# The delta rule of the fourth layer: chunk-sized tiles on quarters of the array, its steps between the projections

## The reference

```python
def gated_deltanet_mixer(h, w_in, conv_w, a_log, dt_bias, o_norm, w_out):
    proj = h @ w_in
    qkv = jax.nn.silu(causal_dwconv(proj[..., :GDN_QKV_W], conv_w))
    ...
    o = gated_delta_chunked(q, k, v.reshape(B, S, GDN_HEADS, GDN_DV), g, beta)
    o = gated_rmsnorm(o, gate.reshape(B, S, GDN_HEADS, GDN_DV), o_norm).astype(h.dtype)
    return o.reshape(B, S, GDN_V_W) @ w_out

# inside gated_delta_chunked, for each chunk of C = 64 tokens
    a = jnp.where(strict, jnp.einsum('nbhid,nbhjd->nbhij', k_beta, kc) * decay, 0.0)
    t_mat = lax.linalg.triangular_solve(a + eye, ...)
    w_val = t_mat @ v_beta
    k_cum = t_mat @ (k_beta * jnp.exp(gc)[..., None])
    attn = jnp.einsum('nbhid,nbhjd->nbhij', qc, kc) * decay
    def step(state, xs):
        v_new = w_i - jnp.einsum('bhcd,bhdv->bhcv', kc_i, state)
        o_i = jnp.einsum('bhcd,bhdv->bhcv', q_i, state) + jnp.einsum('bhij,bhjv->bhiv', at_i, v_new)
        state = state * dl_i[..., None, None] + jnp.einsum('bhcd,bhcv->bhdv', ke_i, v_new)
```

## Time and profile before

| | us |
|---|---|
| median of 3 runs (3168.34 to 3177.97) | 3168.7 |
| the profiled execution | 3162.18 |
| its span, from the first to the last instruction | 3160.9 |
| mean granted TensorE clock | 0.967 of full speed |
| odd mixer in that span | 2168.3 to 2536.5 |

### The profile page before, as it was taken

How to read it: one execution, slowest core, us unless ns; L and a number is a source line. 1 busy time by engine, 2 the same in 40 slices (tenths; PEclk the granted TensorE clock), 3 DMA queues, 4 the chain that set the end, 5 groups by cost and what they waited for, 6 DMA issues and landing times.

```text
span 3160.9 us, 40792 instructions
## 1 busy us (share of the span) xinstructions
PE 2919.8 (92%) x15750; PEld 2079.9 (66%) x15750; DVE 1179.3 (37%) x2588; ACT 480.9 (15%) x1051; POOL 102.7 (3%) x98
## 2 busy tenths in 40 slices
PE   7998899999998899999999999998968789999998
PEld 5666678787666688887755555556868665555554
DVE  2435324433435324442344222225475244222223
ACT  2222301001222311001211111111310111111111
POOL 0000000000000000000010000000000001000000
PEclk9998899999998899999999999999979889999999
DMA  5222146563222146654459999993300229999995
GB/s 186 77 80 74 60 143 242 201 250 106 80 80 80 54 161 240 251 208 157 165 215 395 404 401 400 410 401 139 133 14 1 111 116 409 398 405 404 392 394 228
DMA packets 104979, 684.59 MB, mean 217 GB/s; under 512 B 17760, under 2 KB 19312, under 8 KB 24496
## 3 DMA queue, kind: packets, MB, share of 16 engines
q1 hardware_dynamic: 93040, 665.22, 53.6%
q0 software_dynamic: 11264, 16.54, 1.5%
q10 hardware_dynamic: 576, 1.43, 0.1%
HBM read 703.57 MB, written 4.19 MB: 224 GB/s over the span
## 4 chain that ended last, share of the span: by engine, by line
PE 79%; DMA 10%; DVE 6%; ACT 2%; issue 1%; SPq 0%; DVEq 0%; ACTq 0%; POOLq 0%
PE PS L454 75%; DMA wmoe<-in_experts 10%; PE PS L459 4%; ACT AR L2114 1%; DMA COLS<-in_cols 0%; ACT AR L2164 0%; SPq L2663 0%; DVE wmoe L1826 0%; DVE H L1826 0%; DMA AR<-tokens,IX 0%; ACT ST L2114 0%; DVE ST L1304 0%; DVE wmoe L1324 0%; ACT wmoe L2114 0%; DVE wmoe L1834 0%
## 5 line engine op out<-in xcount | busy, mean ns | idle before, releaser
L454 PE MATMUL PS<-wmoe,AR 128*64 128x256 f32 (+1 forms) x5360 | 716.0, 423 | 33.4 <-DMA wmoe<-in_experts 22.1
L454 PE MATMUL PS<-H,wdense 128*128 128x256 f32 (+1 forms) x3056 | 713.8, 394 | 9.1 <-DVE H L1334 3.6
L454 PEld LDWEIGHTS PS<-H,wdense 128*128 128x128 f32 x3056 | 587.0, 194 | 119.3 <-issue 15.1
L454 PEld LDWEIGHTS PS<-wmoe,AR 128*64 128x64 f32 x5360 | 384.2, 137 | 317.2 <-issue 142.3
L2114 ACT ACTIVATE AR<-PS 128x256 f32<-128x256 f32 (+4 forms) x512 | 231.9, 457 | 1706.6 <-PE PS L454 1100.9
L454 PE MATMUL PS<-AR,wdense 128*128 128x256 f32 (+1 forms) x1920 | 440.4, 389 | 28.9 <-DVE AR L1864 9.8
L454 PE MATMUL PS<-AR 128*128 128x512 f32 (+13 forms) x1492 | 401.4, 408 | 48.3 <-DVE AR L1311 13.8
L454 PEld LDWEIGHTS PS<-AR,wdense 128*128 128x128 f32 x1920 | 367.3, 192 | 95.8 <-issue 20.4
L454 PEld LDWEIGHTS PS<-AR 128*128 128x128 f32 (+6 forms) x1492 | 209.1, 189 | 147.7 <-issue 90.5
L459 PEld LDWEIGHTS PS<-CST,AR 128*128 128x128 f32 (+5 forms) x1158 | 131.8, 135 | 167.1 <-issue 137.8
L454 PE MATMUL PS<-wdense,H 128*128 128x256 f32 (+4 forms) x1024 | 219.7, 371 | 0.0
(11 more groups left out here) (286 smaller groups left out, 1541.6 us busy)
## 6 DMA issues: line engine op xcount, KB each, us to landing
wmoe<-in_experts SPq DMA_DIRECT2D x402, 1024.0 KB, 8.8
wdense<-in_dense SPq DMA_DIRECT2D x176, 1024.0 KB, 4.8
wmoe<-in_ada SPq DMA_DIRECT2D x48, 1024.0 KB, 7.0
tokens<-AR POOLq DMA_DIRECT2D x4, 512.0 KB, 3.4
wdense<-in_dense SPq DMA_DIRECT2D x2, 768.0 KB, 10.5
CST<-in_const SPq DMA_DIRECT2D x1, 1389.0 KB, 19.7
wdense<-in_dense SPq DMA_DIRECT2D x2, 640.0 KB, 6.3
AR<-tokens,IX POOLq DMA_INDIRECT x71, 7.8
```

The costliest lines, as they stand in the source:

```text
L454: return te.matmul(out, lhsT, rhs, start=start, stop=stop, skip_group_check=True)
```

## The change

The tiles of the mixer become half as wide. A matrix of a head is 64 x 64 for each chunk, and the two chunks of a tile lie one above the other on the partitions (`[P, 8, CH]`), so an operation of VectorE or ScalarE covers all eight heads in 512 elements. `by_chunk` forms a product of all heads as 16 products of 64 x 64, chunk 0 on rows and columns 0 to 63 of the array and chunk 1 on rows and columns 64 to 127, into one bank. The masks and identities in the constants are cut to that width.

```diff
+            def by_chunk(what, lhs, rhs, *readers):
+
+                o = bank(what, *readers)
+                for j in range(8):
+                    for r0 in (0, CH):
+                        m = mm(o[r0:r0 + CH, j * CH:(j + 1) * CH], lhs(j, slice(r0, r0 + CH)), rhs(j, slice(r0, r0 + CH)))
+                PE.up(m, *what)
```

```diff
+                for s in range(1, 6):
+                    te.wait_ge(VE.sem, VE.of("ti", t, s - 1))
+                    by_chunk(("ax", t, s), lambda j, r: AM[r, j, :], lambda j, r: TI[r, j, :], AC)
+                    yield
+                    te.wait_ge(VE.sem, VE.of("tt", t, s - 1))
+                    te.wait_ge(AC.sem, AC.of("ax", t, s))
+                    if s < 5:
+                        by_chunk(("ti", t, s), lambda j, r: TT[r, j, :], lambda j, r: XX[r, j, :], VE)
+                    by_chunk(("tt", t, s), lambda j, r: XX[r, j, :], lambda j, r: TT[r, j, :], VE)
+                    yield
+                te.wait_ge(VE.sem, VE.of("tt", t, 5))
+                both = [bank(("kct", t, r), reader(r)) for r in range(2)]
```

```diff
+                    for j in range(8):
...
+                    yield
+                    o = bank(("odd o", t, r), VE)
+                    if n > 0:
+                        te.wait_ge(VE.sem, VE.of("kct", t, 0))
+                        te.wait_ge(AC.sem, AC.of("kct", t, 1))
+                        te.wait_ge(VE.sem, VE.of("state", n - 1))
```

```diff
+    def odd_order(ba, qkv, silu, qk, p0, p1, v0, v1, gate, gated, chunks, out):
+
+        return in_turn((ba, 1), (qkv, 2), (ba, 1), (qkv, 1), (p0, 1), (p1, 1), (qkv, 1), (silu, 1), (p0, 1), (qkv, 1), (p0, 1),
...
-    parts += wide("od_w_in_2", 0, 0, 16) + wide("od_w_in_2", 0, 4096, 1, step=16) + wide("od_w_out_2", 0, 0, 4)
+    parts += wide("od_w_in_2", 0, 4096, 1, step=16) + wide("od_w_in_2", 0, 0, 16) + wide("od_w_out_2", 0, 0, 4)
...
-        sp.wait_ge(PES[1].sem, PES[1].of("kv", 1, 1))
-        sp.wait_ge(VES[1].sem, VES[1].of("kv", 1, 1, 1))
+        sp.wait_ge(PES[1].sem, PES[1].of("odd o", 1, 1))
```

More of the change, by code:

```diff
@@ L928, in odd_mixer @@
         def odd_mixer():
-            steps = feature_steps(("odd qkv",), H, DC, S, 12, lambda j: AC, ("odd h",))
-            run(steps)
-            norms = norm_heads(("odd qk",), 4, [O_MIX[:, 0:4, :], O_MIX[:, 4:8, :]])
-            for j, _ in enumerate(feature_steps(("odd gate",), H, DC, S, 4, lambda j: reader(j))):
-                if j % 2 == 1:
-                    advance(norms, 1)
-            run(norms)
-            slot = take(DC, 16)
-            o = bank(("ba",), VE)
-            for t in range(2):
-                m = sum_k(o[:, 16 * t:16 * t + 16], [H[:, k, t * P:(t + 1) * P] for k in range(DC)], [slot[:, k, :] for k in range(DC)])
@@ new lines, in out @@
+            def out():
+                for n in range(4):
+                    yield
+                    te.wait_ge(AC.sem, AC.of("odd", "squared", n))
+                    o = bank(("odd", "sums", n), AC)
+                    PE.up(mm(o, ones, O_SQ[n % 2]), "odd", "sums", n)
+                    yield
+                    yield
+            nothing = iter(())
+            run(odd_order(decay_inputs(), feature_steps(("odd qkv",), H, DC, S, 12, lambda j: AC), nothing, qk_norms(),
+                          prepare(0), prepare(1), v_turned(0), v_turned(1),
+                          feature_steps(("odd gate",), H, DC, S, 4, lambda j: AC), nothing, chunks(), out()))
@@ L1865, in odd_mixer @@
+            nothing = iter(())
+            run(odd_order(decay_inputs(), convolved(), silu(), qk_norms(), prepare(0), prepare(1), v_turned(0), v_turned(1), nothing,
+                          gated(), chunks(), out()))
             mix_out(L, "odd out")
@@ L2419, in odd_mixer @@
-            norms = norm_heads(("odd qk",), fours[0:4], halves, 1, lambda j: ("silu", 5) if j < 2 else ("odd qk normed", j - 2))
-            for _ in odd_steps(("odd gate",), 8, lambda c, o: (O_GATE[:, c, :], o[:, 0:S])):
-                advance(norms, 1)
-            run(norms)
-            ac.wait_ge(VE.sem, VE.of("ba"))
-            AC.up(act(O_BETA, O_BA[:, :, 0:8], Sigmoid), "beta")
-            ac.preload_act_table_set("natural_log_exp_and_others")
-            AC.up(act(O_EA, row("od_a_log_2", 0, 8), Exp), "decay rate")
@@ L2466, in odd_mixer, with gated @@
-            ac.preload_act_table_set("natural_log_exp_and_others")
+            def gated():
+                for t in range(2):
+                    ac.wait_ge(PE.sem, PE.of("v turned", t, 1))
+                own()
+                for q in range(2):
+                    AC.up(act(O_KV[:, 8 + 4 * q:12 + 4 * q, :], O_GATE[:, 4 * q:4 * q + 4, :], Sigmoid), "odd gate", "sigmoid", q)
+                ac.preload_act_table_set("natural_log_exp_and_others")
+                yield
+                yield
@@ L2467, in odd_mixer @@
+            nothing = iter(())
+            run(odd_order(decay_inputs(), raw(), silu(), qk_norms(), prepare(0), prepare(1), nothing, nothing,
+                          all_steps(("odd gate",), 8, lambda c, o: (O_GATE[:, c, :], o[:, 0:S])), gated(), chunks(), out()))
             layer_norm("odd ln")
```

533 lines of the change are left out of this document (319 added, 214 removed).

## The result

The changed kernel takes 3071.5 us (median of 4 runs, 3070.82 to 3072.53) against 3168.5 for the kernel before on the same chip (4 runs, 3166.02 to 3177.97): a ratio of 0.9689, 95% interval 0.9669 to 0.9709. The forecast was 3047 with a range of 3032 to 3084. The kernel became 97 us faster where 122 were forecast.

The account below looks back on a forecast made before the run. It took the fourth mixer as bound by steps waiting between TensorE and VectorE. Output projection 119.7 us earlier plus 2.4 from its clock gave -122.1 against the 3168.7 median: 3046.6, said as 3047, range 3032 to 3084.

Parts of the forecast that it names:

- Quarter passes at 0.025 us, 38 x 0.80 = 30.4: Solve and what feeds it: 38 groups of 32 quarter passes at 0.80 us each, 30.4 us of TensorE.
- Chunks 33.4 us at full clock: Chunk stage: 16 blocks of 16 passes at 1.8, three sums of 0.86 and 2.0 between array shapes, no wait.
- Beta and decay 6.4, three columns 10.35: Mixer's start: 32 beta and decay passes take 6.4 us, then projection columns at 3.45 us each.
- Output projection 6.9 instead of 9.34: Behind the mixer: first 32 passes, 9.34 us at a lowered clock, take 6.9 with TensorE busy; 2.4 us gained.
- Waits 3.3 and 1.5: TensorE waits 3.3 us before the first solve product, 1.5 before the first state product behind VectorE's two gate multiplies.
- Tail 4.1: After the last chunk output: square, sums, logarithm, exponential and one multiply, 4.1 us before the output projection.
- the seams: Entering another array shape: 0.20 us for about 15 entries before the chunks (3.0), 0.1 for about 20 inside (2.0).
- Vector work of 105 us under 168: Mixer before the chunks: about 105 us of vector work under 168 of TensorE, so VectorE no longer bounds.
- Loads at nothing: Expert weight loads: the later queue wait (89 us instead of 109) and the small beta slot cost nothing.
- B: Rival: two quarters writing one bank do not overlap in the 38 solve groups; +31 us, 3078; chance 0.18.
- C: Rival: late copies or convolutions at about half the solve's twelve hand-overs, 2.5 us each; +15, 3062; chance 0.15.
- D: Rival: small quarter products lower the clock, whole mixer at 1.2 GHz; 237 us more, 3284, slower; chance 0.03.

Follow-up runs that it names:

- the order experiment: Changed kernel with each group's products issued for all heads of tokens 0 to 63 first, then 64 to 127, instead of in pairs: 3092.6 us, ratio 0.9765.

## Why the prediction came out as it did

**The mechanism was right, the clock was not.** The idle time of the solve went, the experts' layer kept its length, the granted clock was 1.00 from 2205 to 2365, and the range held the result. The measured mixer is 98.9 us shorter instead of 119.7, and the output projection behind it gained nothing instead of 2.4. That is 23.2 of the 25 us missing between the medians. The profiled execution's mixer began 11.2 us later than before's, which belongs to the layers ahead (the mixer of the third layer begins 4.9 us later already).

**What the steps measured, against the terms of the sum:**
- *Quarter passes at 0.025 us, 38 x 0.80 = 30.4.* They take 0.031, 0.985 for a group: 37.4, **+7.0**. The row of the third layer held 16 passes in 0.40 us; I take that for too few to see the steady pace, but no run tries it.
- *Chunks 33.4 us at full clock.* From the first state product (2365.38) to the last output product's end (2409.75) it is 44.4, **+11.0**. 16 blocks of 1.86 and three sums of 1.01 would be 32.8, so the work was priced rightly. Low clock in 10.24 + 6.82 + 6.83 = 23.9 us costs half of them, 12. This is the step that failed. It was not among the terms, and "TensorE stays busy now" was taken for enough.
- *Beta and decay 6.4, three columns 10.35.* 8.2 and 13.2, **+4.7**; the clock was low for all but the first 0.1 us until 2193.30, for 5.6 us of the columns.
- *Output projection 6.9 instead of 9.34.* 9.50, **+2.6**. The 2.23 us of idle time and the products on halves ahead of it are still there, and four whole-array products bring 7.17.
- *Waits 3.3 and 1.5.* 2.2 ahead of and within the first level (0.23 + 1.98) and 1.41 ahead of the first state product. The first are right in place and cause. The second is right in place and size, but its cause is another: the two gate multiplies end at 2361.81, and VectorE's copy of the first chunk's values starts at 2364.61 because the copy of the second tile's correction keys, which waits for its product, stands ahead of it. Tail 4.1: 4.1 (2409.75 to 2413.84). These and the seams give back 1.9 of the 22.7 us above, which leaves the 20.8 that the mixer is longer than forecast.
- *Vector work of 105 us under 168.* VectorE waits for others throughout; the convolutions still cost what the earlier trace rows gave.
- *Loads at nothing.* Held.

**The rivals.** B (quarters take turns) is refuted by the order experiment: it would have cost the changed kernel what that one lost, 23 us. C (the queues' order does not hold) is refuted by the 2.2 us of idle time. D named the clock, which is what the forecast lacked, and the wrong place. It looked for a slow clock in the solve's quarters, and those run at 1.00 when they come in pairs, even without a projection between them. Its counterweight was wrong as well: the plain projections are 110 of the 237 us of work, not three quarters. It was also priced as all or nothing over the whole mixer; a few falls in the chunks, worth 12 us, was the case to name.

**What made the gain.** I credited the projections between the steps with covering the waits. Taken out, they cost the mixer 5.6 us of 98.9. The rows say where the gain lies. From the mixer's start to the chunks it is about 67 us (252.9 before, 185.8 after): half-wide matrices in pairs of quarters, five solving levels instead of six, no whole-tile copies. The chunks give about 14 (58.2 to 44.4). Behind them 18 come from the order, since the norm of each chunk and the gate have moved ahead: 22.1 us before, 4.1 after. Within the first part the pairs themselves hold 22.9. The share of each of the others was not tried.

**What stays open.** Why the clock falls in the chunks. Seven profiles show a second and a third fall with no idle time ahead. All 14 begin near the start of the single-quarter block, from 0.44 us before it to 0.71 us into it, so the block can't be what brings them all; ahead of each stand the state and the output product on half of the rows. Nor do they keep step with the blocks: the third fall begins 13.65 us behind the second in all seven, while the starts of the blocks are 13.62 apart in the changed kernel and 13.50 in the experiment on the quarters. That they lie at the same block may follow from a chunk with a fall in it being about as long as that distance. Pairing the block made the falls few and short, but it made one chunk of each tile 1.9 us shorter as well, and the two were not told apart. Nor does such work always bring a fall: the first profile without the idle stretch ran the same half and quarter blocks from 2364.70 to 2392.01 at 1.00. Blocks on halves and quarters of the array without a partner go with falls in most profiles; what decides it in a given execution is not shown.

The first fall needs no single quarter ahead of it. With the block paired and the idle time kept the clock still fell there, for 6.8 us. And it needs no idle time: without the idle stretch both profiles have a first fall all the same (2361.29 and 2361.51), 1.3 and 1.6 us into a single-quarter block.

## What to carry to other kernels

Price a stretch of small products by two questions: are they in pairs that fill different parts of the array, and does anything in it use a half or a quarter alone; TensorE without idle time is not yet TensorE at full clock. Look for products of two independent chunks or tiles that can share a block, since a pair of 128-column products costs what one costs, and the clock fell less in the three profiles that had it. Start a stage with full products and let narrow ones that wait for their input come behind them. And when single executions differ by more than an edit is worth, read the stage's own length in the trace, and do it twice before believing it.

## What the hardware showed that I had not expected

- The clock fell to 0.50 with TensorE busy 6.82 of 6.82 us and all of the 6.8 us ahead of it, behind two blocks on one half of the array's rows. 19.0 us of paired quarters ran at 1.00.
- Two row halves that write different partitions of the same bank work fully at the same time: 32 passes of 128 columns in 1.96 us, as 16 passes alone.
- The fall behind the 1.41 us of idle time lasted longer with more work in it: 6.8 us with the block paired, 10.2 in the changed kernel, 20.5 with whole-array filler right behind the idle stretch. Full work behind the gap did not bring the clock back sooner in that profile.
- A 64-column quarter pass costs 0.050 us alone and 0.031 in a pair, not half of it.
- Narrow products that wait for each piece of their input (16 columns, a pause of 0.26 us between pairs) at the head of the mixer go with a clock of 0.50 for 10.2 or 13.7 us. With two full columns ahead of them it was low for 3.4 us in two profiles and not at all in the third.
